# Input projection of a hybrid encoder layer: memory tile ahead of two row blocks of output weights

## The reference

```
h    = rms_norm(x, g_mix);            proj = h @ w_in          # 1280 tokens x 4096 columns
mix  = concat(hgrn2 heads, differential attention heads)
x    = x + mix @ w_out
x    = x + cross_attention(rms_norm(x, g_ca), rms_norm(mem, g_mem), w_cq, w_ckv, w_co)
x    = x + two-level mixture of experts(...)
```

## Time and profile before

| what | value |
|---|---|
| median of three runs | 1995.02 us (1994.83 to 1995.24) |
| profiled execution, its own time | 1995.95 us |
| its span in the trace | 1994.2 us |
| PE busy | 1905.7 us, 96% of the span |
| DVE busy | 1470.9 us, 74% |
| ACT busy | 1225.4 us, 61% |
| mean granted TensorE clock | 0.983 |
| PE idle between 75 and 200 us | 6.0, 1.8 and 1.0 us |

### The profile page before, as it was taken

The page is one execution under the profiler, slowest core; times in us unless marked ns, Lnnn a source line. Parts: engine busy times, 40 slices in busy tenths (PEclk is TensorE's granted clock), DMA queues, the critical chain, the costliest instruction groups (busy, mean ns, idle before and its releaser), DMA issues.

```text
span 1994.2 us, 33163 instructions
## 1 busy us (share of the span) xinstructions
PE 1905.7 (96%) x11584; PEld 1579.7 (79%) x11584; DVE 1470.9 (74%) x2097; ACT 1225.4 (61%) x1962; POOL 283.6 (14%) x390
## 2 busy tenths in 40 slices
PE   7989999997999899999998999999999999999994
PEld 6868888886888676778887888887888888888882
DVE  5447766777999688777311455578999999999985
ACT  6452577417998698653222333227888888888873
POOL 0220012210000121111000000000222222222210
PEclk9999999998999999999999999989999999999997
DMA  6493334677665631344234322438999999999998
GB/s 202 164 315 120 106 120 145 222 257 222 203 201 181 222 121 62 112 146 145 98 124 161 117 102 90 155 134 293 377 378 389 388 380 378 382 389 379 397 368 329
DMA packets 183961, 452.53 MB, mean 227 GB/s; under 512 B 21088, under 2 KB 105440, under 8 KB 157984
## 3 DMA queue, kind: packets, MB, share of 16 engines
q1 hardware_dynamic: 150448, 346.44, 48.4%
q0 software_dynamic: 33392, 104.50, 14.2%
HBM read 364.88 MB, written 99.61 MB: 233 GB/s over the span
## 4 chain that ended last, share of the span: by engine, by line
PE 43%; ACT 7%; issue 7%; DVE 6%; DVEq 1%; DMA 1%; SPq 1%; ACTq 1%; POOLq 0%
PE cross_ot_ps L113 4%; PE cross_out_ps L113 3%; PE cross_out_ps L115 3%; PE cross_out_ps L114 3%; PE cross_ot_ps L115 3%; PE cross_ot_ps L114 3%; PE amq_banks L113 3%; PE amq_banks L115 3%; PE amq_banks L114 3%; ACT w_w_low L2804 3%; PE amq_banks L2281 2%; PE amq_banks L2262 2%; ACT w_w_high L2804 2%; DVE w_w_low L3037 2%; PE cross_ot_ps L3216 2%
## 5 line engine op out<-in xcount | busy, mean ns | idle before, releaser
L113 PE MATMUL cross_ot_ps<-w_w_high,cross_o_high 128*128 128x512 f32 x528 | 213.5, 404 | 3.9 <-DVE w_w_low L3037 2.1
L115 PE MATMUL cross_ot_ps<-w_w_high,cross_o_low 128*128 128x512 f32 x528 | 207.1, 392 | 0.0
L3037 DVE TENSOR_TENSOR cross_low_up<-cross_raw_up,w_w_high 128x2048 fp32r<-128x2048 f32 x66 | 148.3, 2288 | 9.7 <-ACT w_w_high L2804 9.6
L3037 DVE TENSOR_TENSOR w_w_low<-cross_raw_gate,w_w_high 128x2048 fp32r<-128x2048 f32 x68 | 152.3, 2279 | 0.0
L3037 DVE TENSOR_TENSOR cross_low_down<-cross_raw_down,w_w_low 128x2048 fp32r<-128x2048 f32 x64 | 143.5, 2282 | 0.0
L2804 ACT ACTIVATE w_w_high<-cross_raw_gate 128x2048 fp32r<-128x2048 f32 x68 | 126.2, 1908 | 0.0
L113 PEld LDWEIGHTS cross_ot_ps<-w_w_high,cross_o_high 128*128 128x128 f32 x528 | 99.9, 189 | 29.0 <-DVE w_w_low L3037 6.9
L2804 ACT ACTIVATE w_w_high<-cross_raw_up 128x2048 fp32r<-128x2048 f32 x66 | 122.5, 1907 | 0.3 <-issue 0.3
L2804 ACT ACTIVATE w_w_low<-cross_raw_down 128x2048 fp32r<-128x2048 f32 x64 | 119.0, 1914 | 0.0
L115 PEld LDWEIGHTS cross_ot_ps<-w_w_high,cross_o_low 128*128 128x128 f32 x528 | 99.7, 189 | 21.5
L114 PE MATMUL cross_ot_ps<-w_w_low,cross_o_high 128*128 128x512 f32 x264 | 104.1, 394 | 0.0
(11 more groups left out here) (547 smaller groups left out, 5469.6 us busy)
## 6 DMA issues: line engine op xcount, KB each, us to landing
cross_raw_gate<-in_w_gate_dram SPq DMA_DIRECT2D x66, 1024.0 KB, 7.6
cross_raw_up<-in_w_up_dram SPq DMA_DIRECT2D x66, 1024.0 KB, 9.2
cross_raw_down<-in_w_down_dram SPq DMA_DIRECT2D x64, 1024.0 KB, 8.8
front_pair_raw<-in_w_in_dram SPq DMA_DIRECT2D x9, 1024.0 KB, 7.0
cross_y_kept<-y_rows SPq DMA_DIRECT2D x16, 512.0 KB, 9.6
front_raw<-in_w_in_dram SPq DMA_DIRECT2D x10, 512.0 KB, 5.3
k_t<-front_staged POOLq DMA_DIRECT2D x20, 256.0 KB, 2.6
lf_t<-front_staged_lf POOLq DMA_DIRECT2D x20, 256.0 KB, 2.9
```

The costliest lines, as they stand in the source:

```text
L113: pe.matmul(out, lhs[0], rhs[0], start=first, stop=False)
L115: return pe.matmul(out, lhs[1], rhs[0], start=False, stop=last)
L3037: dve.tensor_tensor(w_low[s][:, cols], raw[s][:, cols], w_high[s][:, cols].bitcast(F32), ALU.subtract).then_inc(w_low_done[s], 1)
```

## The change

In SP's queue tile j+1 of the memory is asked for ahead of blocks 2j and 2j+1 of `w_out`, not behind them. On ACT and DVE the roundings and subtractions of `w_out` that stood last in step n stand in step n+1, behind the memory tile's work and ahead of the sigmoid. On DVE the block of step 9 stands after the loop. PE's and POOL's queues are as they were.

```diff
@@ sync
                 load_chunk(2 * chunks + 1)
+                load_mem(1)
                 for j in range(1, mem_tiles):
-                    load_mem(j)
                     if 2 * chunks + 1 + j < 3 * chunks:
                         load_chunk(2 * chunks + 1 + j)
+                    if j + 1 < mem_tiles:
+                        load_mem(j + 1)
                     load_out(2 * j)
                     load_out(2 * j + 1)
@@ scalar
                     if first_mem <= n < first_mem + mem_tiles:
                         find_mem_rstd(n - first_mem)
+                    for r in out_rounds.get(n - 1, ()):
+                        round_out(r)
                     if kind in SILUS:
                         wide_sigmoid(n)
...
-                    for r in out_rounds.get(n, ()):
-                        round_out(r)
@@ vector
                         scale_mem(n - first_mem)
+                    for r in out_rounds.get(n - 1, ()):
+                        subtract_out(r)
                     wide_silu(n)
-                    for r in out_rounds.get(n, ()):
-                        subtract_out(r)
+                for r in out_rounds.get(first_step[2] - 1, ()):
+                    subtract_out(r)
```

## The result

The changed kernel takes 2008.26 us (median of four runs, 2007.41 to 2009.2) against 1995.13 us (median of four runs; the forecast was reckoned from the 1995.02 us of the first three): a ratio of 1.0063, 95% interval 1.0051 to 1.0074. It is 13.1 us slower. I had forecast slower, by 7.4 us; the range ended at 2006.5. So the direction was right, the size was a little over half of what was measured, and the time lies outside the range. In later repeats of the kernel before, three executions took 2399 to 4899 us in a slow state; they are in no comparison.

The account below looks back on a forecast made before the run. Step 14 was taken to be bound by block 7's landing, which starts S1, whatever PE gains. Landing +5.8 and clock +1.6 gave +7.4 us, 1995.02 to 2002.4 us; range 1993.5 to 2006.5.

Parts of the forecast that it names:

- The gate, S1 plus 27.1 us: DVE to PE: step 14 starts 27.1 us after the landing that starts S1, whatever PE did before.
- The wait that comes in its place: ACT: round_mem waits for the tile's late store in POOL's queue, some 7 us ahead of tile 1.
- The time to landing: Stores of tiles 0, 1, 2: 10.4, 9.4 less 1.0, and 5.7 us to land.
- The discount of 1.0 us: Tile 1's second store: 1.0 us off the 9.4, as tile 3's load is no longer in flight with it.
- The clock: PE, step 14: a slower granted clock after 6.5 us of idle time costs 1.6 us more.
- One to one to the end: PE is never idle from 200 to 400 us, so step 14's shift should reach the end in full.
- A: DMA engines, not the chain, set the end: landing +2 to +3, no clock loss, about 1997.5 us; chance 0.22.
- the rule against the sum: DMA: transfers stood in each other's way at share 0.98, so early loads are out of the way and landing times not constants.
- the second rival: DMA queue that catches up: the late start less the work done in idle time, about 1997.5 us; chance 0.22.
- B: round_mem(1) and round_mem(2): quick landings really remove the wait, S1 allows PE only 1.5 us, 1993.5 us; chance 0.12.
- C: PE's gain goes through, waits and slow clock go: at most 9.4 us, 1985.6, half of it 1990.3; chance 0.06.
- upper end of 2009.1 us: All three memory tile stores take 10.4 us: landing +12.5, with the clock +14.1.

Follow-up runs that it names:

- e3: Changed kernel, but POOL stores the memory tile ahead of the blocks of w_out of the same round: 1994.2 us, ratio 1.0002.
- e4: Changed kernel, but stores to mem_split read the tokens, not the memory tile, so round_mem waits for no store: 2034.9 us, with other data.
- e7: Changed kernel with 36 transposes of the identity in PE's idle time ahead of step 14: 2006.3 us, ratio 1.0047.
- e10: Changed kernel with SP's loads as before, memory tile stored first, w_out blocks dealt out anew, none in step 7: 1987.1 us, ratio 0.9949.
- e8: Changed kernel with mem_split laid out in pieces of 4096 bytes, not 512, its later reads split into four: 2001.3 us, ratio 1.0029.

## Why the prediction was wrong in size

One line of the kernel before is needed here that the earlier trace rows show only as a median, the times to landing of the two stores of tile 2 (issued at 130.5 and 131.3 us):

```profile
DMA to landing us min/median/max: 4.8/5.7/6.6
```

The steps of the prediction, one by one:

- *The gate, S1 plus 27.1 us.* Right, to 0.01 us in eight kernels. It is also why PE's gains in the memory steps counted for nothing.
- *The wait that comes in its place.* Right in kind, in all three places, and shown by e3 and e4. The first start of the late chain was right too: POOL issued tile 0's second store at about 102.3, predicted 102.5.
- *The time to landing.* This is the step that failed. I had taken the times of the earlier trace rows from the issue of the tile's second store: 10.4, 9.4 less 1.0, and 5.7. Measured were 12.1, 10.5 and 7.3, so that the three tiles were rounded at 114.4, 133.4 and 148.0, predicted 112.9, 129.9 and 143.0.
- *What repeats instead.* What nearly repeats, in the three pairs that there are, is not the time since the store's own issue but the time of the whole burst since its first store. Before, the first burst of six ran from 95.73 (the first store of block 0) to 99.91 + 10.4 = 110.3, which is 14.6 us, and the second from 113.48 to 127.2, 13.7 us; after, 99.31 to 114.41, 15.1 us, and 119.86 to 133.35, 13.5 us. The third, of four stores, took 9.6 us before (128.26 to 137.9) and 9.2 after (138.80 to 148.0). Before, POOL had waited for DVE between the blocks and the tile, so the tile's second store left 4.2 us after the first of the burst; now it leaves 3.0 us after it and waits longer for the same bytes.
- *The smaller errors in the same term.* The third time was misread besides: the 5.7 us of the earlier trace rows are the median of tile 2's two stores, and `round_mem(3)` waits for the second, which took 6.6 us (the line above). The discount of 1.0 us for a load that was out of the way was wrong as well: the second burst became 0.2 us shorter. Three times 1.5 to 2.0 us, 5.0 in all, less 1.9 us by which block 5's store landed faster than I had taken (3.9 for 5.8), make up 3.1 of the 9.2 - 5.8 = 3.4 us by which S1 was later than forecast (172.1, where I had said 167 to 170). That these two errors are opposed is luck.
- *The clock.* 1.6 us predicted, 1.6 measured and shown by e7. The idle time ahead of step 14 was 4.0 and not 6.5 us, since PE came later than I had thought; 4.0 was enough. I had taken the 1.6 us from an idle time of 6.0 us, so that they fit a shorter one is in part luck.
- *One to one to the end.* 10.8 us at the end of step 14 became 13.1 in the median. I had no term for the other 2.3 us, and can't say that there is one: the profiles scatter by more than that in this part, and the cause stays open.
- *The rivals.* A (a queue that catches up; the rule against the sum means it by "the second rival") held that shares near 1 leave no room. It had the last landing 2 to 3 us late, and it was 9.2. The share fell to 0.81, with idle windows between the bursts: the chain of waits is the bound. B and C fell because the wait for the store was there to its full length. A gain as in B is to be had, but it needs POOL's and SP's queues to be changed as well (e10).

Why the time lay outside the range is only in part this step. With the landings as measured the sum would be 9.2 + 1.6 = 10.8 us, so 2005.8 us, just inside; the rest of the way to 2008.3 us is the part after step 14 that stays open. I had an upper end of 2009.1 us in the text, with all landings at 10.4 us, and cut the range at 2006.5. Two of three landings were at or above that 10.4.

## What to carry to other kernels

When work is moved within the queue of one engine, draw the queues of the others that were left as they are: POOL still stored the blocks first, so a tile that was finished 2.5 us before the first of them was held back behind them, and a single buffer made a wait of 8.6 us of it. A landing time read from a trace belongs to its place in a burst; if the burst gets denser, keep the time of the burst and not that of the transfer (here it kept within 0.5 us in three pairs). And before a stall is removed, look for the next gate behind it (here the sum S1): in e4 PE was relieved and idle again 60 us later.

## What the runs showed of the hardware

- Stores in pieces of 512 bytes take longer than the same bytes in pieces of 4096: the first burst went from 15.1 to 12.9 us (e8), and issuing a tile's store took POOL 0.53 us, where the median had been 0.96. The rate in a single window shows less. From 107 to 110 us the engines were occupied 99% at 247 GB/s in the changed kernel, but in e8 too they were at 100% and 270 GB/s there; from 104 to 107 us it was 337 against 399 GB/s. What else slows the later window is not shown. The Trainium skill (Perfetto Trace Analysis, DMA Optimizations) says that DMAs below 2 KB have a marked overhead each. Here each DMA is 512 KB and only its pieces are short, and for these the runs point the same way.
- An idle time of PE of 3.5 us (e8) or 4.0 us (the changed kernel) ahead of step 14 was followed by a stretch at the lower clock that cost 1.6 us, the same as after 6.0 us in the kernel before. An idle time of 2.7 us (e8, ahead of step 9) was not followed by one: the granted clock was 1.00 from 133 to 145 us. The transposes right behind the idle time do not tell: in e4, after 4.0 us ahead of step 9, they took 1.09 us as at full clock, and yet the matmuls from 128.9 to 131.9 us lasted 0.63 us in place of 0.39, at a granted clock of 0.87 over 127 to 140 us.
